# Eight column tiles of a modulation vector: from TensorE in the up projection to VectorE in the down projection

## What is computed

```python
# first block, end
f = conv_ffn(x_mid * (1 + sc2) + sh2, w_up, dw_w, dw_b, w_down, b_down)   # D_FF = 2816
x = layer_norm(ALPHA * x_mid + g2 * f, ln2_g, ln2_b)
# second block
mod = silu(c_2) @ ada_w + ada_b                 # [1024] @ [1024, 6144]
sh1, sc1, g1, sh2, sc2, g2 = split(mod, 6)
h = rms_norm(x, norm1_g) * (1 + sc1) + sh1      # sh1, sc1: needed first
...                                             # attention and RWKV branches on h
x = x + g1 * (mixed @ w_out)
h2 = rms_norm(x, norm2_g) * (1 + sc2) + sh2
x = x + g2 * moe_ffn(h2, ...)
```

## Time and profile before

| | |
|---|---|
| median of 3 runs | 2343.19 us (2342.17 to 2351.72) |
| profiled execution, first to last instruction | 2343.3 us |
| TensorE busy | 2151.4 us, 92% |
| VectorE busy | 1330.6 us, 57% |
| ScalarE, GpSimd busy | 461.2 us, 396.7 us |
| mean granted TensorE clock | 0.973 of full speed |
| moved by DMA | 446.60 MB, mean 191 GB/s |

### The profile page before, as it was taken

The page is one execution under the profiler, slowest core; times in us unless marked ns, Lnnn a source line. Parts: engine busy times, 40 slices in busy tenths (PEclk is TensorE's granted clock), DMA queues, the critical chain, the costliest instruction groups (busy, mean ns, idle before and its releaser), DMA issues. The chain is left out here.

```text
span 2343.3 us, 27600 instructions
## 1 busy us (share of the span) xinstructions
PE 2151.4 (92%) x10395; PEld 1246.3 (53%) x10395; DVE 1330.6 (57%) x2524; ACT 461.2 (20%) x916; POOL 396.7 (17%) x771
## 2 busy tenths in 40 slices
PE   6999989999999999999879999998699999999975
PEld 3444554777785458883443788445333333333322
DVE  3448863766672134434968333535766766767745
ACT  2013561121120011004235232011011111111111
POOL 0005000111000000000000000000444444444433
PEclk9999999999999999999989999998799999999988
DMA  9422000535524015981111100401499999898976
GB/s 389 180 81 81 36 1 20 233 144 216 215 81 179 36 72 229 391 306 54 37 57 58 51 3 4 177 36 54 180 372 397 425 353 421 344 407 357 413 281 252
DMA packets 68999, 446.60 MB, mean 191 GB/s; under 512 B 12276, under 2 KB 12932, under 8 KB 44066
## 3 DMA queue, kind: packets, MB, share of 16 engines
q0 software_dynamic: 36176, 254.42, 27.1%
q1 hardware_dynamic: 32722, 190.78, 21.0%
HBM read 416.27 MB, written 73.45 MB: 209 GB/s over the span
## 5 line engine op out<-in xcount | busy, mean ns | idle before, releaser
L965 PE MATMUL psum<-arena 128*128 128x256 f32 x1904 | 416.7, 381 | 2.1 <-PEq L1005 2.0
L2824 PE MATMUL psum<-arena 128*64 128x512 f32 (+1 forms) x1088 | 366.1, 600 | 38.9 <-DVE arena L2872 16.6
L965 PEld LDWEIGHTS psum<-arena 128*128 128x128 f32 x1904 | 361.4, 190 | 62.6 <-issue 14.0
L2872 DVE STREAM_TRANSPOSE arena<-arena 32x256 f32<-32x256 f32 x832 | 362.1, 435 | 15.8 <-DMA arena<-scratch_h,arena 4.1
L2824 PEld LDWEIGHTS psum<-arena 128*64 128x64 f32 (+1 forms) x1088 | 143.8, 165 | 226.6 <-issue 197.7
L2815 PE MATMUL psum<-arena 128*64 128x512 f32 (+1 forms) x544 | 186.2, 598 | 1.2 <-ACT arena L2850 1.2
L1067 PE MATMUL psum<-arena 128*128 128x512 f32 x352 | 151.8, 592 | 0.3 <-PEq L1091 0.3
L2815 PEld LDWEIGHTS psum<-arena 128*64 128x64 f32 (+1 forms) x544 | 68.5, 163 | 113.2 <-issue 111.8
L869 PE MATMUL psum<-arena 128*128 128x512 f32 x256 | 111.2, 593 | 2.3 <-DVE arena L2432 1.5
L1067 PEld LDWEIGHTS psum<-arena 128*128 128x128 f32 x352 | 66.6, 190 | 83.4 <-issue 83.4
L2878 DVE COPY arena<-psum 128x512 f32<-128x512 f32 x51 | 35.3, 692 | 132.7 <-PE psum L2815 132.7
(11 more groups left out here) (521 smaller groups left out, 2932.0 us busy)
## 6 DMA issues: line engine op xcount, KB each, us to landing
scratch_expert_out<-arena SPq DMA_DIRECT2D x18, 2048.0 KB, 19.9
scratch_expert_out<-arena SPq DMA_DIRECT2D x51, 512.0 KB, 9.9
arena<-in_w_ada SPq DMA_DIRECT2D x12, 2048.0 KB, 16.8
arena<-in_ada_w POOLq DMA_DIRECT2D x12, 2048.0 KB, 8.8
arena<-in_w_up SPq DMA_DIRECT2D x22, 1024.0 KB, 4.8
arena<-in_w_in SPq DMA_DIRECT2D x9, 2048.0 KB, 11.0
arena<-in_w_down SPq DMA_DIRECT2D x5, 2048.0 KB, 8.6
arena<-in_w_o SPq DMA_DIRECT2D x2, 2048.0 KB, 8.4
```

The source lines that it names most:

```text
L965: last = pe.matmul(out, w[:, k, :], x[:, k, :], start=(k == 0), stop=(k == KH - 1))
L2824: last = pe.matmul(K.bank[2 + s][r, :], xt[:, s, P * k + r.start:P * k + r.stop], gu[:, lane, 2 * E_FF * k:2 * E_FF * (k + 1)], start=(k = ...
L2872: last = dve.transpose(channels[c:c + 32, :, a:a + 32], tokens[a:a + 32, :, c:c + 32])
```

## The change

Modulation tiles 0 to 3 (shift and scale of the next norm) stay with TensorE in up tiles 4 to 7. Tiles 4 to 11 leave the up projection. Their weights are loaded by GpSimd in 32 units of 128 x 1024 (512 KB, two of a tile's eight row blocks side by side) through a ring of four slots in the first half of the modulation stage; the first four are loaded at the end of the up phase. In the down projection VectorE multiplies each block of 128x512 with its 128 values of silu(c_2), one to a partition, and adds up the eight blocks of a tile: 24 units before the first row tile's chain, four behind the chain of row tile 0 and four behind that of row tile 1. Within the last row tile, TensorE sums all eight results over the partitions by eight matmuls with a matrix of ones of 32 columns, tile 4g + j into bank g, partitions 32j to 32j + 31. VectorE adds the bias and applies the gain behind the chain of row tile 2, in the compact form (four rows of 1024 in the four quarters of the partitions). SP stores the rows with two transfers, behind its last weight stream. `gated2`, `arow` and `sel_rows` go; `down_tile` hands out lists of slices in place of a three-dimensional view, with the same addresses.

```diff
+def weigh_rows(dve, acc, rows, vec, signal):
+    for k, row in rows:
+        if k == 0:
+            link(dve, dve.tensor_scalar(acc, row, vec[:, k, 0:1], None, ALU.mult), signal)
+        else:
+            link(dve, dve.scalar_tensor_tensor(out=acc, in0=row, scalar=vec[:, k, 0:1], in1=acc, op0=ALU.mult, op1=ALU.add), signal)
+ADA2_FIRST, ADA2_RING = 4, 4
+ADA2_UNITS = 4 * (ADA_TILES - ADA2_FIRST)
+def ada2_unit(K, pool, u):
+    w = K.dram["ada_w_2"][ADA2_FIRST + u // 4]
+    K.unit_in[u % ADA2_RING].by(pool.dma_start(K.ada2[:, 0, D * (u % ADA2_RING):D * (u % ADA2_RING) + D], w[:, D * (u % 4):D * (u % 4) + D]), 16)
...
 # phase_modulate, VectorE
-            sel_done.by(dve.tensor_copy(K.sel_rows[:, :], K.sel[:, 0:1].to_broadcast([P, P])))
...
 # phase_ffn_up, TensorE (ScalarE's copies likewise)
-                if 1 <= j <= ADA_TILES:
+                if 1 <= j <= ADA2_FIRST:
                     ada_end(j - 1)
-                if 0 <= j < ADA_TILES:
+                if 0 <= j < ADA2_FIRST:
                     pe.wait_ge(a2in[j % 2].sem, 16 * (j // 2 + 1))
                     pe.wait_ge(a2copy.sem, j)
                     a2mm.by(ada_products(pe, K.bank[6], aw[:, j % 2, :], K.vec2))
...
 # phase_ffn_up, VectorE
-                modulation(n - 1 - FIRST - 1)
-                if n == late + 2:
-                    dve.wait_ge(n2in.sem, 16)
-                    link(dve, dve.tensor_scalar(K.arow[:, 2, :], K.arow[:, 2, :], 1.0, None, ALU.add), K.dve_step)
-                    link(dve, dve.tensor_tensor(K.arow[:, 2, :], K.arow[:, 2, :], aw[:, 0, 0:D], ALU.mult), K.dve_step)
...
 # phase_ffn_up, GpSimd
-            a2bias.by(pool.dma_start(K.arow[:, :, :].rearrange("p a n -> p (a n)"), d["ada_b_2"].rearrange("a b n -> (a b n)")[2 * D:6 * D].partition_broadcast(P)), 16)
...
-            pool.wait_ge(a2mm.sem, ADA_TILES)
-            n2in.by(pool.dma_start(aw[:, 0, 0:D], d["norm2_g"].partition_broadcast(P)), 16)
+            pool.wait_ge(a2mm.sem, ADA2_FIRST)
+            for u in range(ADA2_RING):
+                ada2_unit(K, pool, u)
...
 # phase_ffn_down, TensorE
+                    if t == NT - 1 and n == 2:
+                        pe.wait_ge(weighed.sem, 2 * ADA2_UNITS)
+                        pe.wait_ge(moved.sem, 2 * KD)
+                        for g in range(2):
+                            for j in range(4):
+                                rows = pe.matmul(K.bank[g][32 * j:32 * j + 32, :], K.ones[:, 0:32], acc[:, 4 * g + j, :], start=True, stop=True)
+                        row_mm.by(rows)
...
             def in_ahead(blocks):
+                pe.wait_ge(rows_ready.sem, 1)
                 pe.wait_ge(moved.sem, 2 * KD)
...
 # phase_ffn_down, SP
-            spilled.by(sp.dma_start(d["mod_rows"], K.arow[0:1, :, :]), 16)
-            sp.wait_ge(spilled.sem, 16)
             stream(K, sp, d["w_in2"][0])
             stream(K, sp, d["w_in2"][1])
+            sp.wait_ge(rows_ready.sem, 1)
+            halves = d["mod_rows"].rearrange("a (b n) -> (a b) n", n=512)
+            for g in range(2):
+                K.spilled.by(sp.dma_start(halves[4 * g:4 * g + 4, :], K.row[0:P:32, 3, 512 * g:512 * g + 512]), 16)
...
 # phase_ffn_down, GpSimd
+            for u in range(ADA2_RING, ADA2_UNITS):
+                pool.wait_ge(weighed.sem, 2 * (u - ADA2_RING + 1))
+                ada2_unit(K, pool, u)
+            for slot, (to, src) in enumerate(((ring[:, 0, :], d["ada_b_rows"]), (gain, d["norm2_g_rows"]))):
+                pool.wait_ge(weighed.sem, 2 * (ADA2_UNITS - ADA2_RING + slot + 1))
+                extra_in.by(pool.dma_start(to, src), 16)
...
 # phase_ffn_down, VectorE
+            def weigh(units):
+                for u in units:
+                    dve.wait_ge(K.unit_in[u % ADA2_RING].sem, 16 * (u // ADA2_RING + 1))
+                    weigh_rows(dve, acc[:, u // 4, :], [(2 * (u % 4) + i, ring[:, u % ADA2_RING, 512 * i:512 * i + 512]) for i in range(2)], K.vec2, weighed)
+            weigh(range(24))
             for t in range(NT):
...
+                if t < 2:
+                    weigh(range(24 + 4 * t, 28 + 4 * t))
+                if t == 2:
+                    dve.wait_ge(row_mm.sem, 1)
+                    dve.wait_ge(extra_in.sem, 32)
+                    link(dve, dve.tensor_tensor(made, K.psum[:, 0:D], bias, ALU.add), K.dve_step)
+                    rows_ready.by(dve.scalar_tensor_tensor(out=made[0:64, 512:D], in0=made[0:64, 512:D], scalar=1.0, in1=gain[0:64, :], op0=ALU.add, op1=ALU.mult))
...
 # next phase, SP, at its end
+            sp.wait_ge(K.spilled.sem, K.spilled.n)
```

More of the change, by code:

```diff
@@ L1058, in phase_output, with down_tile @@
     K.memory.release("gated", "cat")
+def down_tile(K, pe):
+    slot = take(K, pe)
+    return [slot[:, D * k:D * k + D] for k in range(4)]
 def down_products(K, pe, t, n, w, first=False, last=False):
@@ L1083, in phase_ffn_up @@
     rows = lambda n: K.hmid[:, n + 1:n + 3, :]
-    late = FIRST + ADA_TILES
+    late = 16
     conv = lambda n: (K.hmid[:, n, :], value[n % 3] if n < late else aw[:, 1, T * (n - late):T * (n - late) + T])
     a2in = [K.dma_signal("ada2_landed0"), K.dma_signal("ada2_landed1")]
-    a2bias, n2in = K.dma_signal("ada2_bias"), K.dma_signal("norm2_g_landed")
-    a2mm, a2copy, a2cols, a2rows, a2out = (sig(n) for n in ("ada2_used", "ada2_copied", "ada2_columns", "ada2_rows", "ada2_rows_out"))
+    K.unit_in = [K.dma_signal(f"ada2_unit_landed{i}") for i in range(ADA2_RING)]
+    a2mm, a2copy, a2cols, a2out = (sig(n) for n in ("ada2_used", "ada2_copied", "ada2_columns", "ada2_columns_out"))
     col_bank = K.bank[7][:, 0:32].rearrange("p (m v) -> p m v", v=2)
@@ L1095, in ada_end @@
                 pe.wait_ge(a2copy.sem, j + 1)
[L1096 to L1101, removed]
+                a2cols.by(ada_columns(pe, K.bank[7], K.part[:, j % 2, :], K.sel[:, :], j))
             t1, t2, t4 = K.h_mixed
@@ L1133, in _ @@
                     a2mm.by(ada_products(pe, K.bank[6], aw[:, j % 2, :], K.vec2))
[L1135 removed]
+            K.down_first = down_tile(K, pe)
             pe.wait_ge(done.sem, 4)
[L1137 removed]
+            pe.wait_ge(a2out.sem, 1)
             down_products(K, pe, 3, 0, K.down_first, first=True)
@@ L1288, in phase_ffn_down @@
     per = 4
-    spare, early_in = sb("w_down_early", [P, per * D + (NF - 5 * per) * D]), sig("w_down_early_landed")
-    spilled = K.dma_signal("mod_rows_in_dram")
-    early = {2: spare[:, 0:per * D].rearrange("p (k n) -> p k n", n=D), 5: spare[:, per * D:].rearrange("p (k n) -> p k n", n=D)}
+    spare, ends, early_in = sb("w_down_early", [P, per * D]), [sb(f"w_down_end{i}", [P, D]) for i in range(2)], sig("w_down_early_landed")
+    K.spilled = K.dma_signal("mod_rows_in_dram")
+    weighed, row_mm, rows_ready = sig("ada2_weighed"), sig("ada2_rows_summed"), sig("mod_rows_ready")
+    extra_in = K.dma_signal("ada2_bias_landed")
+    ring, acc = K.ada2[:, 0, :].rearrange("p (u n) -> p u n", n=D), K.ada2[:, 1, :].rearrange("p (j n) -> p j n", n=512)
+    bias, gain, made = ring[:, 0, :], ring[:, 1, 0:512], K.row[:, 3, :]
+    gated = [made] * (NT - 1) + [K.ada2[:, 1, 0:D]]
+    early = {2: [spare[:, D * k:D * k + D] for k in range(per)], 5: ends}
     with nc.Block() as block:
@@ L1296, in _ @@
             for n in range(2):
-                w = take(K, pe).rearrange("p (k n) -> p k n", k=per) if n else K.down_first
+                w = down_tile(K, pe) if n else K.down_first
                 for t in range(NT) if n else (1, 2):
@@ L1307, in _ @@
                     if t == 0 and n in (3, 4):
-                        late[n] = take(K, pe).rearrange("p (k n) -> p k n", k=per)
+                        late[n] = down_tile(K, pe)
                     last = down_products(K, pe, t, n, late[n] if n in (3, 4) else early[n], last=(n == order[-1]))
@@ L1331, in _ @@
         def _(sp):
-            early_in.by(sp.dma_start(spare[:, 0:per * D], d["w_down"][2]), 16)
-            early_in.by(sp.dma_start(spare[:, per * D:], d["w_down"][5][:, 0:(NF - 5 * per) * D]), 16)
+            early_in.by(sp.dma_start(spare[:, :], d["w_down"][2]), 16)
+            for i, end in enumerate(ends):
+                early_in.by(sp.dma_start(end[:, :], d["w_down"][5][:, D * i:D * i + D]), 16)
             for n in (3, 4):
                 stream(K, sp, d["w_down"][n])
-            spilled.by(sp.dma_start(d["mod_rows"], K.arow[0:1, :, :]), 16)
-            sp.wait_ge(spilled.sem, 16)
             stream(K, sp, d["w_in2"][0])
             stream(K, sp, d["w_in2"][1])
+            sp.wait_ge(rows_ready.sem, 1)
+            halves = d["mod_rows"].rearrange("a (b n) -> (a b) n", n=512)
+            for g in range(2):
+                K.spilled.by(sp.dma_start(halves[4 * g:4 * g + 4, :], K.row[0:P:32, 3, 512 * g:512 * g + 512]), 16)
         @block.gpsimd
```

42 lines of the change are left out of this document (15 added, 27 removed).

## The result

| | before | after |
|---|---|---|
| median | 2342.68 us (2341.51 to 2351.72, 4 runs) | 2326.04 us (2316.5 to 2327.73, 4 runs) |
| profiled execution | 2343.3 us | 2324.6 us |
| TensorE busy | 2151.4 us | 2138.3 us |

What follows compares the result with a forecast made beforehand. TensorE was taken to bound the up projection with and without modulation, and to run the down projection nearly without gaps. -23.3 + 1.9 = -21.4 us from the 2343.19 median gave 2321.8 us, range 2318 to 2328.

Steps and rivals of the forecast that it cites:

- rival 2: End of down projection: late constant row or slow addition costs 1 to 5 us, time 2323 to 2327; chance 0.08.
- rival 1: Down projection: slow ring loads starve VectorE; mild 2326, chance 0.03; hard, loads one at a time, 2376, chance 0.02.
- Out of the up projection, -23.3: Up projection: eight tiles lose their modulation products and row sum, 15.00 to 12.09 us each, saving 23.3 us.
- rival 3: Up projection doesn't speed up because VectorE or the weight stream binds at 15 us; time 2345.1, chance 0.02.
- Into the down projection, +1.9: Last row tile: TensorE's eight matmuls of 32 columns add 1.9 us; the remaining row work stays covered.
- The ring: Down projection: four-slot loads on GpSimd's queue feed VectorE in time, landing in 3.7 us; stall taken as 0.
- r: Microseconds per unit in the down projection: larger of 1.58 and (landing + 1.9)/4; TensorE stalls from 3.66 up.
- The room of 65.5: Down projection: VectorE is free for 65.5 us before the first sum, to hold the first 24 units.
- the estimate of 5.1 us a unit: Down projection: by the skill's fixed 2.0 us per transfer, loads strictly one after another; stall 40, time 2362.
- The stall rule: Down projection: TensorE stalls only if the first 24 units take more than 79.1 us.
- the row sums' wait for ScalarE's copies: Last row tile: transposed rows written by 859.8, needed at 869.1, so no wait was expected.
- The step that failed: Up projection: removing ScalarE copies, VectorE additions, the norm-gain fold and the bias broadcast is worth 0.

Runs made afterwards that it cites:

- experiment 5: Changed kernel without its down part: no units loaded or weighed, the eight row sums left out, rows holding only bias and gain; 2326.36 us.
- experiment 7: Changed kernel with a ring of one slot in place of four; 2420.9 us, one of four runs left out of the ratio 1.0316.
- experiment 6: Changed kernel with every unit weighed three times, twice into a spare buffer; 2367.92 us.
- experiment 8: Changed kernel with a ring of two slots in place of four; 2337.98 us.
- experiment 1: The changed kernel measured once more, nothing edited; 2325.34 us.
- experiment 2: Changed kernel with an unused 2048 KB broadcast where the bias load stood in GpSimd's queue; 2321.37 us.
- experiment 4: Kernel before the change with only its bias load moved to up tile 3; 2346.38 us against 2343.71.
- experiment 9: Changed kernel, GpSimd's row and residual work four up tiles later, its first two modulation weight loads behind up tiles 0 and 1; 2318.72 us, repeated 2324.08.

## Why the prediction was right

The direction and the two stages of the sum were right. That the total fell into the range was in part luck: the 4.2 us above the sum are where the prediction had put its rival 2 (2323 to 2327) and the mild form of rival 1 (2326), and neither happened. A term that it had put at 0 filled their place.

- *Out of the up projection, -23.3*: right, -23.2. The tiles ran at 12.09 in places 8 to 15 too; rival 3 falls.
- *Into the down projection, +1.9*: right, +2.06 (experiment 5). The row sums and the addition kept their cover: 1.66 us of idle time where 1.3 was forecast. Rival 2 falls.
- *The ring*: the outcome was right, the size of a term wrong. I took the landing of 3.7 us and with it VectorE as the pace, 37 us for 24 units. Landings were 6.1 us and r 2.64, and the units ended at 58.8 us. This is near the 60 us for a landing of 8.8, but by other terms: a first wait of 9.22 us and 2.18 a unit. The argument against rival 1 was wrong as well (the stage carries 91 GB/s, and only its first dozen microseconds share the engines with other loads). The ring's own bytes and SP's weight streams kept them busy for 0.91 of the 58.75 us, at 335 GB/s. The room of 65.5 held all the same. The Trainium skill's fixed part per transfer ("DMA: Bandwidth & Descriptors", "Anatomy of one DMA") doesn't decide here: the estimate of 5.1 us a unit was for loads one after another, and with four in flight a unit takes 2.64. With one in flight (experiment 7) it takes 6.6, and the kernel is slower than before; how much of this is the fixed part, no run here shows. The stall rule, 79.1 us and then microsecond for microsecond, gave the first gap of experiments 6, 7 and 8 within 0.1 us. For longer stalls it lacked a term: the row sums' wait for ScalarE's copies (8.39 and 10.87 us), of which the prediction said that it had long come true.
- *The step that failed*: ScalarE's copies, VectorE's additions "and the 2048 KB bias broadcast on GpSimd's queue; TensorE never waited for them, so they are worth 0". The broadcast was worth a loss: while it stood there it held back the rows behind it, and so GpSimd's work. Without it that work starts 5.6 us earlier, beside VectorE's operations for which TensorE waits, and makes the larger gap: 2.75 us (experiment 1 against 2, where a useless load in its place takes the gap away). The head as a whole lost more, 4.1 us in experiment 1 and 5.8 in the first profile, for the smaller gap and the lower clock add to it; for these the broadcast is not shown to be the cause. My question there was who waited for the transfer; it should have been what started when it was done.
- *The total*: -23.2 + 2.1 + 4.1 (experiment 1's head) = -17.0, against the medians' -16.6 and, in experiment 1, -18.4.

Open: why the granted clock falls behind the same gap of 2.5 to 2.7 us in some executions (after, ring of two) and not in others (experiments 1, 4, 5, 6 and the ring of one); what sets VectorE's wait for `w_up` in the head. It is 1.55 us in the kernel before, without a gap, 1.77 to 1.84 us in three executions with a smaller gap of 0.29 to 0.37, 2.26 us in experiment 4 with 0.78, and 2.85 to 3.00 in five with 1.35 or 1.36; experiment 9 removes wait and gap. Whether the change has a part in it, no run shows.

## What to carry to other kernels

A transfer for which nobody waits is not free to remove: look at what is queued behind it, when that will start instead, and beside which work of the bottleneck's feeders it will then stand. To move work under a bottleneck's shadow, work out the deadline of the engine that receives it (here 79.1 us for a unit count) and give the loads as many slots as hide their landing, counted with the bytes that they themselves add to the stage. And where a change of 20 us is to be priced in a program of 2300, set it against the old kernel with the same side effects, by the starts of the same instructions.

## What the runs showed of the hardware

- GpSimd's additions and products on SBUF tiles stretch VectorE's operations with two SBUF inputs: four side taps from 3.11 to between 5.09 and 6.33 us, two gates from 1.29 to 3.44, one sum of weights from 0.69 to 1.41. An operation with one input in PSUM kept its 0.69 us in the midst of it (L985 in experiment 2). The Trainium skill ("SBUF — State Buffer", "Who interferes with whom") tells of just this, that a VectorE instruction with two SBUF inputs contends with a GpSimd instruction that reads SBUF; the trace agrees.
- Behind TensorE gaps of 2.53, 8.39 and 29.40 us the granted clock was 0.67, 0.56 and 0.56 over the next 5 us or so, and behind a gap of 2.60 us in another execution 1.00. The first of these cost 1.7 us beyond its gap (88 records in 20.92 us instead of 19.23).
- A 512 KB load landed, at the median, after 4.1 us in a ring of one slot, 4.4 in a ring of two and 6.1 in a ring of four, and made its user wait up to 13.6 us beside the down weights. It is not the slots alone: with four slots and each unit weighed three times (experiment 6) the median was 4.1 again.
